# A fused transformer block on one core: 22 sums of w_down quarters made by transfers in DRAM, and two more gate/up blocks as seven half-size products

## What is computed

```python
h = rms_norm(x); proj = h @ w_in          # split into q, k, v, f, u, cv, cb, cc and gates g
y_a = forgetting_attention(q, k, v, f) @ w_proj_attn     # 8 heads of 64, causal
y_b = multiscale_pool(u) @ w_proj_pool
y_c = short_gated_conv(cv, cb, cc) @ w_proj_conv
x = x + (gates[0] * y_a + gates[1] * y_b + gates[2] * y_c) @ w_out
h = rms_norm(x); a, b = split(h @ w_gate_up)             # FFN_HIDDEN = 2816, 22 blocks of 128
x = x + (silu(a) * b) @ w_down                           # w_down is 2816 x 1024
out = rms_norm(x)
```

## Time and profile before

| | us |
|---|---|
| median of 3 runs | 773.13 (772.8 to 773.3) |
| the profiled execution, its own time | 774.61 |
| its span, first to last instruction | 772.8 |
| TensorE busy | 762.9 (99%) |
| VectorE busy | 649.2 (84%) |
| ScalarE busy | 420.6 (54%) |
| GpSimd busy | 18.3 (2%) |

### The profile page before, as it was taken

One profiled execution on the slowest core, in us unless ns is written; L12 is line 12 of the kernel. 1 busy time (PEld: TensorE's weight loads), 2 busy tenths in 40 slices (PEclk: granted clock), 3 DMA queues, 4 the chain that ended last, 5 costly groups with the idle time before them and its releaser, 6 DMA issues.

```text
span 772.8 us, 12216 instructions
## 1 busy us (share of the span) xinstructions
PE 762.9 (99%) x4451; PEld 677.7 (88%) x4451; DVE 649.2 (84%) x1041; ACT 420.6 (54%) x712; POOL 18.3 (2%) x41
## 2 busy tenths in 40 slices
PE   8999999999999999999999999999999999999997
PEld 7888888888889999999978888999999998888885
DVE  6788876767798969777777899899999985799997
ACT  5626556647544546455445744555555552655554
POOL 2001101100000000000000000000000000000001
PEclk9999999999999999999999999999999999999999
DMA  8862542323133443344376533333333365353422
GB/s 296 271 220 76 174 105 69 91 54 100 42 105 82 110 121 98 83 110 113 106 265 198 192 98 93 110 111 109 97 100 106 110 196 159 128 172 122 151 96 110
DMA packets 133311, 99.46 MB, mean 129 GB/s; under 512 B 5932, under 2 KB 114532, under 8 KB 133252
## 3 DMA queue, kind: packets, MB, share of 16 engines
q1 hardware_dynamic: 132596, 98.35, 42.2%
q10 hardware_dynamic: 144, 0.26, 0.1%
q0 software_dynamic: 512, 0.07, 0.1%
HBM read 90.21 MB, written 8.39 MB: 128 GB/s over the span
## 4 chain that ended last, share of the span: by engine, by line
PE 96%; DVE 2%; issue 1%; DMA 1%; ACT 0%; POOL 0%; POOLq 0%; DVEq 0%
PE bank L913 10%; PE bank L917 10%; PE bank L915 10%; PE bank L1349 7%; PE bank L1347 7%; PE bank L1345 7%; PE bank L1161 4%; PE bank L1400 4%; PE bank L1159 4%; PE bank L1401 4%; PE bank L1399 4%; PE bank L1157 4%; PE bank L1195 2%; PE bank L1196 2%; PE bank L1197 2%; PE bank L1258 1%
## 5 line engine op out<-in xcount | busy, mean ns | idle before, releaser
L913 PE MATMUL bank<-operands,whi 128*128 128x512 f32 x352 | 138.2, 393 | 0.7 <-DVE wlo L2076 0.7
L917 PE MATMUL bank<-operands,wlo 128*128 128x512 f32 x352 | 137.3, 390 | 0.0
L915 PE MATMUL bank<-operands,whi 128*128 128x512 f32 x352 | 137.2, 390 | 0.0
L2076 DVE TENSOR_TENSOR wlo<-raw,whi 128x1024 fp32r<-128x1024 f32 x61 | 74.3, 1223 | 16.4 <-ACT whi L1465 15.7
L913 PEld LDWEIGHTS bank<-operands,whi 128*128 128x128 f32 x352 | 66.2, 188 | 14.3 <-DVE wlo L2076 1.1
L1465 ACT CAST whi<-raw 128x1024 fp32r<-128x1024 f32 x61 | 63.9, 1052 | 26.9 <-PE bank L917 8.3
L917 PEld LDWEIGHTS bank<-operands,wlo 128*128 128x128 f32 x352 | 66.1, 188 | 13.9
L915 PEld LDWEIGHTS bank<-operands,whi 128*128 128x128 f32 x352 | 66.2, 188 | 13.2
L1349 PE MATMUL bank<-sums_hi,wlo 128*128 128x256 f32 x240 | 68.0, 283 | 0.0
L1347 PE MATMUL bank<-sums_lo,whi 128*128 128x256 f32 x240 | 68.0, 283 | 0.0
L1345 PE MATMUL bank<-sums_hi,whi 128*128 128x256 f32 x240 | 68.0, 283 | 0.0
(11 more groups left out here) (323 smaller groups left out, 2001.8 us busy)
## 6 DMA issues: line engine op xcount, KB each, us to landing
raw<-in_w_in_dram SPq DMA_DIRECT2D x105, 256.0 KB, 3.3
raw<-in_w_gate_up_dram SPq DMA_DIRECT2D x88, 256.0 KB, 3.3
raw<-in_w_down_dram SPq DMA_DIRECT2D x53, 256.0 KB, 3.0
big_x<-in_x_dram SPq DMA_DIRECT2D x8, 512.0 KB, 5.0
tiles<-in_w_out_dram SPq DMA_DIRECT2D x4, 1024.0 KB, 7.4
w_sums<-tiles SPq DMA_DIRECT2D x4, 1024.0 KB, 7.2
raw<-w_sums SPq DMA_DIRECT2D x16, 256.0 KB, 3.1
raw<-in_w_out_dram SPq DMA_DIRECT2D x12, 256.0 KB, 3.7
```

The source lines that it names most:

```text
L913: nc.tensor.matmul(banks[b][:, 0:width], whi[:, s, w], op(hi + k * S), start=a, stop=False)
L915: nc.tensor.matmul(banks[b][:, 0:width], whi[:, s, w], op(lo + k * S), start=False, stop=False)
L917: mm = nc.tensor.matmul(banks[b][:, 0:width], wlo[:, s, w], op(hi + k * S), start=False, stop=z)
L2076: nc.vector.tensor_tensor(wlo[:, s, :], raw[:, s, :], whi[:, s, :].bitcast(F32), ALU.subtract).then_inc(w_lo, 1)
```

## The change

It adds a DRAM tensor `down_sums` (2 x 1408 rows of 512 floats). In each of the four pairs GpSimd issues one transfer of 2.88 MB from `w_down` in DRAM into it: a copy in pairs 0 and 2, an adding transfer in pairs 1 and 3 (each after its copy has landed). This gives the 11 sums of the first pass and the 11 of line 2913. The down stage loads them (`down_sum(0)` straight into `chain(r)`, `down_sum(1)` into `raw`), and `first_sum` and line 2913 are gone. Blocks 19 and 20 become turns; `ffn_last` is block 21 alone. The read-back of `x2_kept` moves from `ffn_last` to the loads r = 6 to 9 of the down stage. The sums of tiles 0 and 1 move into the last turn. The load r = 3 now waits for `used >= NU`, since `chain(3)` lies over an operand of `ffn_last`.

```diff
-          ("ffn_first", 1, 2), ("ffn_head", 1, 6), ("turns", 1, 105),
-          ("ffn_last", 1, 6), ("down", 1, 77)]
+          ("ffn_first", 1, 2), ("ffn_head", 1, 6), ("turns", 1, 119),
+          ("ffn_last", 1, 2), ("down", 1, 77)]
-TURNS = range(4, 19)
+TURNS = range(4, 21)
+        down_sums = nc.dram_tensor("down_sums", [2 * FH // 2, D // 2], F32, kind="Internal").ap()
...
+        def down_sum(kind):
+            return down_sums[kind * R * P:(kind + 1) * R * P, :]
...   SP: x2_kept is no longer read in ffn_last
+            sp.wait_ge(down_added, 32)
             for r in range(R):
-                if r == SPARE:
+                if r == SLOTS:
                     sp.wait_ge(used, NU)
-                elif r == SPARE + SLOTS:
+                if r == 0:
+                    sp.wait_ge(used, turn_part(LAST_TURN, F22) + 1)
+                if r == SPARE + SLOTS:
                     sp.wait_ge(w_lo, NU + 2 * (SPARE - SLOTS) + 2)
-                else:
+                elif r < SLOTS - LAST_UNITS:
+                    turn_raw_read(LAST_UNITS + r)
+                elif r != SPARE:
                     sp.wait_ge(w_lo, NU - SLOTS + r + 1 if r < SLOTS else NU + 2 * (r - SLOTS) + 2)
-                load_down(r, [(2 * r, 1), (2 * r, 0)])
+                load_down(r, [(down_block(2 * r, 1), down_raw(r, 0)),
+                              (down_sum(0)[r * P:(r + 1) * P, :], chain(r))])
+                if SPARE <= r < SPARE + TB:
+                    t = r - SPARE
+                    sp.dma_start(big_x[:, t * D:(t + 1) * D], x2_kept[t * P:(t + 1) * P, :]
+                                 ).then_inc(x2_back, 16)
...   POOL, in the loop over pairs i, behind the f_pair transfers
+                kind, adds = i // 2, i % 2
+                down = w_down.rearrange("(r e p) c -> p r e c", e=2, p=P)
+                to = down_sum(kind).rearrange("(r p) c -> p r c", p=P)
+                if not adds:
+                    pool.dma_start(to, down[:, :, 0, (1 - kind) * HALF:(2 - kind) * HALF]
+                                   ).then_inc(down_copied, 16)
+                else:
+                    pool.wait_ge(down_copied, 16 * kind + 16)
+                    pool.dma_start(to, down[:, :, kind, 0:HALF], accum_op=ALU.add
+                                   ).then_inc(down_added, 16)
...   PE
+            pe.wait_ge(turn_gates, 2 * LAST_TURN)
+            pe.wait_ge(turn_posted, 4 * LAST_TURN)
             gate_up("ffn_last", 0, 0)
             pe.wait_ge(turn_gates, 2 * len(TURNS))
             pe.wait_ge(turn_posted, 4 * len(TURNS))
-            for j in range(1, 3):
-                gate_up("ffn_last", 0, j)
...   ACT
                 act.wait_ge(*landed_down(r))
                 parts_hi(NU + 2 * r, down_raw(r, 0))
-                act.wait_ge(summed, r + 1)
                 parts_hi(NU + 2 * r + 1, chain(r))
...   DVE
-            def first_sum(r):
-                dve.wait_ge(*landed_down(r))
-                if r == 3:
-                    dve.wait_ge(used, NU)
-                nc.vector.tensor_tensor(chain(r), down_raw(r, 0), down_raw(r, 1),
-                                        ALU.add).then_inc(summed, 1)
...
-                b12, b22 = raw[:, s, 0:HALF], raw[:, s, HALF:2 * HALF]
-                nc.vector.tensor_tensor(b12, b12, b22, ALU.add).then_inc(summed, 1)
+                b22 = raw[:, s, HALF:2 * HALF]
                 nc.vector.tensor_tensor(chain(r), chain(r), b22, ALU.add).then_inc(summed, 1)
```

More of the change, by code:

```diff
@@ L78 @@
     "v_lo_part": dict(pair=2),
-    "vector_step": dict(norm=11, front=23, pair=5, mix=6, rounds=8, ffn_first=3, ffn_head=5, turns=7, ffn_last=4,
+    "vector_step": dict(norm=11, front=23, pair=5, mix=6, rounds=8, ffn_first=3, ffn_head=5, turns=10, ffn_last=1,
                         down=3),
@@ L599, in load @@
                     sp.sem_inc(loads_begun, 1)
[L600 to L604, removed]
+                elif stage == "ffn_last":
+                    s = last_slot(j)
+                    turn_raw_read(j)
                     sp.sem_inc(loads_begun, 1)
@@ L616, in load, with turn_raw_read @@
                                  ).then_inc(landed[s], 16)
+            def turn_raw_read(m):
+                v, part, sums = ((-2, F22, 3), (-1, F21, 4), (-1, F22, 3))[m]
+                v += len(TURNS)
+                sp.wait_ge(w_lo, turn_part(v, part) + 1)
+                sp.wait_ge(turn_summed, 4 * v + sums)
             def columns(w, col):
@@ L769, in _ @@
                                      ).then_inc(landed[s], 16)
[L770 to L778, removed]
@@ L781, in load_down, with down_block @@
-            def load_down(k, blocks):
+            for n, c in enumerate(gate_up_columns(TURNS[-1] + 1)):
+                load("ffn_last", 0, n, c)
+            def down_block(row, c):
+                return w_down[row * P:(row + 1) * P, c * HALF:(c + 1) * HALF]
+            def load_down(k, parts):
                 signal = spare_in if k == SPARE else landed[k % SLOTS]
[L784 to L787, removed]
+                for src, to in parts:
+                    sp.dma_start(to, src).then_inc(signal, 16)
@@ L1310, in gate_up @@
             def gate_up(stage, i, j):
-                a = (2 * j + 2) % 6
+                a = (2 * j + 2) % 6 if stage == "ffn_head" else 0
                 k = j // 3 + 1
@@ L1457, in split_hi @@
                 n, s = unit(stage, i, j)
-                act.wait_ge(landed[s], 32 * loads_before(stage, i, j))
+                from_slot = last_slot(j) if stage == "ffn_last" else s
+                act.wait_ge(landed[from_slot], 32 * loads_before(stage, i, j))
                 if stage == "out" and j < SLOTS:
                     act.wait_ge(used, weight_part(len(ROUNDS) - 1, (T1, B22, T4)[j]) + 1)
-                elif stage == "ffn_last" and j < SLOTS:
-                    act.wait_ge(used, turn_part(len(TURNS) - 1, (F1, F22, F4)[j]) + 1)
+                elif stage == "ffn_last":
+                    act.wait_ge(used, turn_part(LAST_TURN, (F1, F22, F4)[j]) + 1)
                 elif not (stage == "front" and n < SLOTS):
                     act.wait_ge(used, n - SLOTS + 1)
-                nc.scalar.copy(whi[:, s, :], raw[:, s, :]).then_inc(w_hi, 1)
+                nc.scalar.copy(whi[:, s, :], raw[:, from_slot, :]).then_inc(w_hi, 1)
             def operand_hi(dst, src, scale=1.0):
@@ L2859, in _ @@
                 turn_post(v, 3, 3, 2, u, 1)
-                if last:
+                if not last:
+                    turn_lo(v + 1, F2, turn_sum(0, 2), 2)
+                else:
                     split_lo("ffn_last", 0, 1)
-                else:
-                    turn_lo(v + 1, F2, turn_sum(0, 2), 2)
+                    hid_sum(0)
+                    wait_free(dve, 1, "ffn_head", 0, 1)
+                    hid_sum(1)
                 dve.wait_ge(used, turn_part(v, F22) + 1)
@@ L2869, in _ @@
             turn_hidden(len(TURNS) - 1)
-            split_lo("ffn_last", 0, 2)
             def second_lo(r):
```

81 lines of the change are left out of this document (35 added, 46 removed).

## The result

The changed kernel takes **777.82 us** (median of 4 runs, 777.7 to 779.2) against 773.06 for the kernel before (772.8 to 773.3): ratio 1.0062, 95% interval 1.0048 to 1.0075. It is slower, by 4.8 us.

A forecast was written before the change was run, and what follows sets the result against it. TensorE, busy 762.9 of 772.8 us, was taken as the bound, its time a count of matmuls from 478 us. Turns gave -1.6, all other parts 0: 773.13 - 1.6 = 771.5 us; 8-in-10 range 771.0 to 778.0.

The forecast's parts named there:

- the four DRAM transfers: GpSimd's copies and adds in the pairs: TensorE loss taken as 0; if the whole add goes first, 6 to 16 us.
- turns by packets: Rival at SP's stores: engines alternate packets, so the whole add is served first; 777.7 us, or 787 us; chance 0.21.
- When the add moves: First add in the pairs: copy begun at 74.3 seen landed at 88 or 89, add moving data from about 90 us.
- What is free: Slack behind the second w_sums store: 2.0 us before ScalarE's line 1468 plus 1.4 in the chain to pair 1's logits, 3.4 us.
- the prediction's own rule: At pair 1's logits, TensorE loses only what the second store is late by more than 3.4 us.
- the add going first: Sign for the rival with the whole add served first: pair 1's logits start at 119 or later; rival's chance 0.21.
- The add's own length: DRAM transfers: 10 to 19 us taken for an add, 10 us for a copy.
- Room elsewhere: Second copy from 119 us, second add from 151: DMA engines 28% busy, latest-issued load has 12.1 us; room for both.
- Blocks 19 and 20 as turns: TensorE before the down stage: 21.77 us of whole blocks replaced by 20.16 us of turns, 1.61 us less.
- The sums off VectorE: Down stage: 22 sums, 15.0 us, taken off VectorE; worth 0 because TensorE waits for nothing there.
- VectorE's busy time: Sign over the kernel: some 3 us less, 15.0 off by the sums and some 12 on by the two turns.
- Start of the down stage, x2: Later load r = 3 and x2 read-back among loads r = 6 to 9: cost 0 each, bound 1 us each.

The follow-up runs named there:

- e11: The changed kernel with each add cut by rows into four pieces, packets still 2 KB, copies unchanged; 783.35 us, ratio 1.0137.
- e8: The changed kernel with both copies moved to pair 2 and both adds to pair 3, away from the w_sums stores; 779.00 us, ratio 1.0078.
- e6: The kernel before with the 22 sums made by DRAM transfers, adds held until the w_sums stores landed, blocks 19 and 20 whole; 773.50 us, ratio 1.0009.
- e3: The changed kernel without the DRAM transfers, VectorE making the 22 sums again, blocks 19 and 20 still turns; 773.31 us, ratio 1.0003.
- e4: The changed kernel with a plain copy in place of the first add, so the first sums lack their second term; 778.74 us, ratio 1.0070.

## Why the prediction was wrong, point by point

The step that failed is that of the four DRAM transfers: "*I take 0: it is the end that needs no more than a share in favour of the queue that has three or four transfers waiting against one, but it is nearly a toss.*" There is no such share. A DMA engine gives each queue one packet in turn (63 to 64, 81 to 81, 199 to 197), so a queue with four transfers waiting gets no more than one with a single transfer, and one with small packets gets less: of 0.21 MB per us SP's loads had 0.04. The right mechanism, turns by packets, stood among the rivals with 0.21; its argument against itself, that the add starts late and part of the stores is through, didn't hold, since the second store had barely begun. But that its 777.7 lies so near 777.82 is luck. It took all 88 packets of the add per engine to go first and the store to be 9.6 us late. The loads ahead of the store were through by then, only some 40 of the 88 went before the store's end, and it was 7.7 us late; the clock and the logits, in nobody's sum, made up the difference.

- *When the add moves:* about 90 forecast; 92 seen, for an issue at 85.98. The profile of the kernel after starts up 1.6 us earlier (`f_pair` at 80.34 for 81.94), so that is 93.6 in the forecast's count. Those 3.6 us helped: a start 1 us earlier meets the loads too (e11).
- *What is free:* 3.4 us forecast. The store landed at about 102.9. With the same 1.6 us that is 7.7 us later than the 96.8 of the earlier trace rows, less the 3.4: 4.3 us of TensorE by the prediction's own rule. In the trace it stands for 3.29 us, and of the 6.58 lost some 1.7 us more are the clock: seven matmuls at 0.43 us for 0.227, and a slower one at either end. The logits behind them, with small gaps of their own, take 1.4 more. What a gap costs after its end was in no term of the sum. Pair 1's logits began at 116.86, 118.5 in the forecast's count, close to the sign named for the add going first (119).
- *The add's own length:* 10 to 19 us taken; the first landed 26.6 us after its issue, the second 21.3. Of these some 6 and 3 pass before data move; they moved for some 19.5 and 17.5 us, so the upper bound was near. The copy's 10 were 12.9 to landing.
- *Room elsewhere:* "there is room: loads of the pairs keep the DMA engines 28% busy" was right in its result, as the second add cost nothing, but not in its reason. e8 shows the same place without room for two adds in a row. The lead of 12.1 us lasts for one add; how long a lead lasts at the rate that is left was not asked.
- *Blocks 19 and 20 as turns:* -1.61 forecast, -1.60 in the trace.
- *The sums off VectorE:* "worth 0. It can't be worth more, since no wait is there to go". Right by itself (e6), wrong in the sum: without it the turns' 1.6 us are eaten by new gaps (e3). The trace of before had the warning in it, VectorE at 10.0 of 10.0 us in the down stage with its sums.
- *VectorE's busy time:* some 3 us less forecast, 0.5 less seen (649.2 to 648.7): a size off, without weight for the sum.
- *Start of the down stage, x2:* no wait of TensorE after 478 us in the kernel after; right.

Freed of the meeting with the stores, the rest of the sum holds to half a microsecond: 771.71, 771.87 and 771.95 against 771.5, or 1.0 to 1.3 us under the kernel before of the same series where 1.6 were forecast. What is missing is about the 0.6 us that e6 lost with the sums alone; its cause stays open.

## What to carry to other kernels

A background transfer is not free because the DMA engines are idle 70% of the time: while it runs, every other queue gets one packet for each of its packets, so price it by packets (those of your own queue up to the end of what you wait for, times the sum of both durations, over 16 engines: for the store 512 x 0.274 / 16 = 8.8 us, a little above the 8.0 that 64 per us make), and give it small packets or a place where nothing urgent is queued. Ask also how long the foreground's lead lasts at that rate. And relief for an engine that has no waits can be worth 0 alone and still be what another part of the change needs.

## What the runs showed of the hardware

- Once both queues move, arbitration is one for one between GpSimd's and SP's at every mix of sizes seen: 63:64 (2 KB and 2 KB), 81:81 (2 KB and 512 bytes), 117:115 (512 bytes and 2 KB), 199:197 (512 and 512), 87:84 (4 KB and 512). For 1 to 2 us behind the first packets of a transfer on GpSimd's queue SP's gets next to nothing (76:5, and 91:0 in e4).
- A 2 KB packet of an add from DRAM to DRAM takes 0.176 us of an engine, a 512-byte one about 0.064, a 4 KB one of a copy 0.160; a 2 KB packet of the store from SBUF 0.098 beside it. A 512-byte load packet takes some 0.027 us alone and 0.041 beside an add's.
- An add issued at 85.98 moved data only from 92 on, 6 us later; the second, issued at 158.65 with SP's queue empty, from 161 on. With packets waiting on SP's side, 1 us of this start went with 5 us of the end (e11).
- After a gap of 3.29 us TensorE's granted clock fell to its lower level within a few matmuls, and the stretch of 5.7 us shows 0.70; after 5.4 us (e8) it was low from the first (two matmuls of 256 columns 0.38 us apart, for 0.12).
